# Recurrence blocks opened early, beside products and in a head lane's bank, with attention heads dealt seven and five

## The reference

```python
z = h @ w_in
za, zb, zc = jnp.split(z, [3 * A_WIDTH, 3 * A_WIDTH + 2 * B_WIDTH], axis=-1)
oa = dilated_attention(q, k, v, rel_bias_table)      # 12 heads of 64
ob = spatial_gating(zb, norm_gain, w_s, b_s)         # gelu, layernorm, a 128x128 product per group
oc = rwkv7_time_mix(zc, ...)                         # 12 heads of 64, two to a block of 128 channels: 6 blocks
return jnp.concatenate([rmsnorm(oa), rmsnorm(ob), oc], axis=-1) @ w_out
```

```python
zc = zc + (prev - zc) * mu                           # shift by one token
w_log = -softplus(-(w0 + tanh(w_lo) @ w_up)) - 0.5
decay = exp(-exp(w_log))
a = sigmoid(a0 + a_lo @ a_up)
kk = normalize(k * k_k);  k = k * (1.0 + (a - 1.0) * k_a)
state = state * w_t + sa * (kk_t * a_t) + v_t * k_t;  y_t = state @ r_t
y = layernorm per head(y) * ln_gain + ln_bias + sum(r * k * r_k) * v
return y * g
```

## Time and profile before

| what | us |
|---|---|
| median of three runs | 2358.93 |
| the profiled execution's own time | 2356.4 |
| its span (first to last instruction) | 2354.7 |
| TensorE busy | 2267.6 |
| last stages of products, ST_VB on | 218.75 to 338.24 |
| mixer, first opening | 338.24 to 365.72 |
| mixer, levels to output, blocks 0 to 2 | 365.72 to 452.46 |
| mixer, second opening | 452.46 to 474.48 |
| mixer, levels to output, blocks 3 to 5 | 474.48 to 557.58 |
| last finishes and splits, to the first product of ST_OUT | 557.58 to 565.19 |

### The profile page before, as it was taken

The page is one execution under the profiler, slowest core; times in us unless marked ns, Lnnn a source line. Parts: engine busy times, 40 slices in busy tenths (PEclk is TensorE's granted clock), DMA queues, the critical chain, the costliest instruction groups (busy, mean ns, idle before and its releaser), DMA issues.

```text
span 2354.7 us, 31774 instructions
## 1 busy us (share of the span) xinstructions
PE 2267.6 (96%) x13038; PEld 1971.1 (84%) x13038; DVE 1359.6 (58%) x1694; ACT 1066.1 (45%) x1375; POOL 58.2 (2%) x66
## 2 busy tenths in 40 slices
PE   8999989899989999999999999999998999999998
PEld 7888978788877888888888888888986889889776
DVE  5444657476566766667676444755445555545554
ACT  4433433323455545454555333545435453544543
POOL 0000020011000000000000000000000000000000
PEclk9999998899999999999999999999999999999999
DMA  7656520013634555555565555554550556445243
GB/s 276 198 173 217 185 89 1 1 32 115 220 114 144 191 183 193 182 194 181 194 199 196 193 189 191 191 191 128 186 179 19 179 179 221 161 149 169 68 128 140
DMA packets 235977, 373.07 MB, mean 158 GB/s; under 512 B 8359, under 2 KB 108244, under 8 KB 235092
## 3 DMA queue, kind: packets, MB, share of 16 engines
q1 hardware_dynamic: 229740, 362.89, 46.9%
q10 hardware_dynamic: 6120, 8.50, 1.0%
HBM read 369.25 MB, written 2.12 MB: 158 GB/s over the span
## 4 chain that ended last, share of the span: by engine, by line
PE 65%; issue 5%; DVE 4%; ACT 2%; POOL 0%; DVEq 0%; POOLq 0%; ACTq 0%
PE PS L466 16%; PE PS L425 12%; PE PS L427 12%; PE PS L426 12%; PE PS L469 8%; DVE w_lo L343 1%; PE PS L1960 1%; ACT w_hi L338 1%; PE PS L2050 1%; PE PS L2034 1%; PE PS L1944 1%; PE PS L905 1%; DVE small L1998 0%; PE PS L2725 0%; ACT spare L1972 0%
## 5 line engine op out<-in xcount | busy, mean ns | idle before, releaser
L343 DVE TENSOR_TENSOR w_lo<-raw,w_hi 128x2048 fp32r<-128x2048 f32 (+2 forms) x340 | 766.4, 2254 | 760.5 <-ACT w_hi L338 760.3
L338 ACT ACTIVATE w_hi<-raw 128x2048 fp32r<-128x2048 f32 (+2 forms) x340 | 641.2, 1886 | 850.9 <-PE PS L427 491.3
L466 PE MATMUL PS<-h_both,w_hi 128*128 128x512 f32 x1968 | 536.5, 394 | 2.9 <-DVE h_both L922 1.8
L425 PE MATMUL PS<-w_hi,h_both 128*128 128x512 f32 (+2 forms) x1344 | 514.8, 383 | 11.3 <-DVE h_both L922 4.6
L426 PE MATMUL PS<-w_lo,h_both 128*128 128x512 f32 (+2 forms) x1344 | 507.2, 377 | 0.0
L427 PE MATMUL PS<-w_hi,h_both 128*128 128x512 f32 (+2 forms) x1088 | 408.0, 375 | 0.0
L466 PEld LDWEIGHTS PS<-h_both,w_hi 128*128 128x128 f32 x1968 | 336.5, 188 | 47.4 <-DVE h_both L922 2.8
L469 PEld LDWEIGHTS PS<-h_both,w_lo 128*128 128x128 f32 x1968 | 301.2, 188 | 42.9
L469 PE MATMUL PS<-h_both,w_lo 128*128 128x256 f32 x1968 | 313.1, 281 | 0.0
L425 PEld LDWEIGHTS PS<-w_hi,h_both 128*128 128x128 f32 x1344 | 254.0, 189 | 59.1 <-DVE h_both L922 5.1
L426 PEld LDWEIGHTS PS<-w_lo,h_both 128*128 128x128 f32 x1344 | 254.2, 189 | 45.5
(11 more groups left out here) (523 smaller groups left out, 2045.0 us busy)
## 6 DMA issues: line engine op xcount, KB each, us to landing
raw<-in_w_in SPq DMA_DIRECT2D x132, 1024.0 KB, 5.1
raw<-in_ffn_w_up SPq DMA_DIRECT2D x176, 512.0 KB, 4.3
raw<-in_w_out SPq DMA_DIRECT2D x48, 1024.0 KB, 5.1
raw<-in_ffn_w_down SPq DMA_DIRECT2D x44, 1024.0 KB, 5.0
raw<-in_mem_wkv SPq DMA_DIRECT2D x8, 1024.0 KB, 11.7
raw<-in_mem_wq SPq DMA_DIRECT2D x4, 1024.0 KB, 5.5
raw<-in_mem_wo SPq DMA_DIRECT2D x4, 1024.0 KB, 7.4
raw<-in_w_in SPq DMA_DIRECT2D x4, 768.0 KB, 4.5
```

What stands on the lines that cost most here:

```text
L338: act.activation(w_hi[:, slot % 2, :st.n], raw[:, slot, :st.n], ACT.Copy).then_inc(hi_made, 1)
L343: dve.tensor_tensor(w_lo[:, slot % 2, :st.n], raw[:, slot, :st.n], w_hi[:, slot % 2, :st.n].bitcast(F32), ALU.subtract).then_inc(lo_made, 1)
L425: pe.matmul(ps, l_hi, r_hi, start=start, stop=False, skip_group_check=skip)
L466: pe.matmul(sums, wh[:, k, cs], h_both[:, :, kk, :], start=kk == 0, stop=False, skip_group_check=True)
```

## The change

The opening of a block becomes a job of its own (`open_tensor`, `open_scalar`, `open_vector`, kept in `rk_opens`), and a recurrence block has 19 rounds.

- Openings of blocks 0, 1, 2 are woven in beside products, starting two rounds apart (`EARLY`), in PSUM banks 6, 7 and 5. For this `prepare_*` begins with ST_VB and makes a whole shift per round in another order (`SHIFTS`), the spatial gating starts four rounds after it, and parts of the low-rank weights are loaded early by four more transfers on ScalarE's queue. Evacuations of ST_QK and ST_V0 wait for openings whose scratch room they overwrite (`qk_scalar` and its like).
- Openings of blocks 3, 4, 5 are the first three jobs of head lane 1, six rounds each, in that lane's bank 3: rounds 0 to 17 of the mixer.
- Heads are dealt 0 to 6 to lane 0 and 7 to 11 to lane 1. Lane 0 then has finishes 0 and 2 (rounds 35 to 42), lane 1 has head 11 in rounds 38 to 42, `a_norm` in 43 and finish 1 in 44 to 47. The recurrence lanes have 38 rounds, 0 to 37. The pauses and the early putting aside of four heads are gone.
- Masks are loaded during the last product stage to other places, and GpSimd zeroes the recurrence's matrices and writes their diagonals after one of the last two units.

```diff
+def rounds(n):
+    for _ in range(n):
+        yield
+def after(n, part):
+    yield from rounds(n)
+    yield from part
+def spaced(part, pauses):
+    for n in pauses:
+        yield from rounds(n)
+        next(part, None)
+        yield
...
-        SHIFTS = (18, 15, 12, 0, 3, 6, 9)
+        SHIFTS = (6, 12, 15, 18, 9, 0, 3)
+        V_BANK = 4
...
-        MASKS, PAIR = 6144, 7426
-        GUP, YT, LE = 4096, 6144, (5632, 7680)
-        LNG, LNB = 0, C_W
+        MASKS, PAIR = 5632, 5632
+        GUP, YT, LE = 4096, 6144, ((sp_, 6144), (rw, 7680))
+        LNG, LNB = 4608, 21248
...
+            o = Steps(open_chain if inside else lane["chain"], **OPEN)
...
+            o.room = early_rooms[b] if o.first else dict(kk=lane["kk"], a=lane["a"], L=lane["L"], E=lane["E"],
+                                                         u0=late_u[b - 3][:, 0, :], u1=late_u[b - 3][:, 1, :])
+            o.bank = (6, 7, 5)[b] if o.first else OPEN_BANK
...
+        def qk_scalar(act, q):
+            if q.c == 2:
+                act.wait_ge(rk_opens[0].dve, rk_opens[0]["al"])
+            qk_to_scalar(act, q)
...
+        EARLY = (0, 2, 4)
+
+        def opened(part, e, pauses):
+            return together(*[after(n, spaced(part(e, rk_opens[b]), pauses)) for b, n in enumerate(EARLY)])
+
+        def opened_tensor(pe):
+            return opened(open_tensor, pe, (1, 2, 2, 1))
...
         def recur_tensor(pe, j):
...
-            pe.matmul(PS[:, A, 0:S], raw_flat[0:HD, LORA + j.b * P:LORA + (j.b + 1) * P], zc[0:HD, 18, :], start=True,
-                      stop=True).then_inc(j.pe, 1)
...
-            pe.wait_ge(j.dve, j["al"])
+            pe.wait_ge(j.o.dve, j.o["al"])
...
-        HEADS_FIRST, TO_FIRST, TO_SECOND, HEAD_ROUNDS = 8, 3, 5, 5
-        LANE_JOBS = [[Pause(TO_FIRST)] + side_jobs[0:HEADS_FIRST:2] + [Pause(TO_SECOND)] + side_jobs[HEADS_FIRST::2]
-                     + [finishes[0], finishes[2]],
-                     [Pause(TO_FIRST)] + side_jobs[1:HEADS_FIRST:2] + [Pause(TO_SECOND)] + side_jobs[HEADS_FIRST + 1::2]
-                     + [a_norm, finishes[1]]]
-        PUT_FIRST = (0, 1, HEADS_FIRST, HEADS_FIRST + 1)
+        LANE_JOBS = [side_jobs[:HEADS_FIRST] + [finishes[0], finishes[2]],
+                     [rk_opens[b] for b in range(3, CB)] + side_jobs[HEADS_FIRST:] + [a_norm, finishes[1]]]
...
+        def later_tensor(pe, j):
+            yield from spaced(open_tensor(pe, j), (0, 0, 1, 0))
+            yield
...
-            for st in (ST_C, ST_CE, ST_VB):
+            for st in (ST_C, ST_CE):
                 run(products_tensor(pe, st))
-            fill = prepare_tensor(pe)
-            weave(products_tensor(pe, ST_B1), fill)
-            fill = together(fill, gating_tensor(pe))
-            weave(products_tensor(pe, ST_QK), fill)
-            weave(products_tensor(pe, ST_V0), fill)
+            fill = together(prepare_tensor(pe), after(4, gating_tensor(pe)), after(4, opened_tensor(pe)))
+            for st in (ST_VB, ST_B1, ST_QK, ST_V0):
+                weave(products_tensor(pe, st), fill)
             run(fill)
             mixer(pe, recur_tensor, side_tensor)
...
+            act.dma_start(z_v[0:HD, 0, 0:3 * P], I["rwkv_w_up"][0][:, 0:3 * P]).then_inc(lora_early, 16)
+            act.dma_start(z_v[HD:P, 0, 0:3 * P], I["rwkv_a_up"][0][:, 0:3 * P]).then_inc(lora_early, 16)
...
+            for n, (lane, zero) in enumerate(zip(rk_lanes, zeros)):
+                pool.wait_ge(unit_used, ST_V0.U1 - (2 if n == 0 else 1))
+                pool.memset(lane["mats"], 0.0).then_inc(zero.pool, 1)
...
-            sp.wait_ge(unit_used, ST_V0.U1)
-            sp.dma_start(sp_(MASKS, 8 * P), I["masks"][:, 0:8 * P]).then_inc(masks_in, 16)
+            sp.wait_ge(sgu.dve, sgu["nsq1"])
+            sp.dma_start(ar(MASKS, 8 * P), I["masks"][:, 0:8 * P]).then_inc(masks_in, 16)
+            sp.wait_ge(lo_made, ST_V0.U1 - 1)
```

More of the change, by code:

```diff
@@ L1057, in prepare_scalar @@
         def prepare_scalar(act):
[L1058 to L1061, removed]
+            yield from rounds(4)
+            act.wait_ge(prep.dve, prep["m3"])
             act.activation(zc[0:HD, 18, :], zc[0:HD, 18, :], ACT.Tanh).then_inc(prep.act, 1)
@@ L1163, in gating_vector @@
             st = sgu_stats
-            for n in range(2):
-                yield
-                yield
-            yield
+            yield from rounds(6)
             for t_ in range(TB):
@@ L1266, in hybrid_two_blocks @@
         rk_jobs = {}
+        open_chain = Chain(new, "rk_open")
+        OPEN_BANK = 3
+        OPEN = dict(pe="low lora nsum nbc bonus0 bonus", act="sig_e sig_a sq nb end f0 f1 g0 g1 h0 h1 hh", pool="npow",
+                    dve="l0 l1 kk ka kmod nmax kkn ru akk plus minus end0 end1 bon be kE rg al")
+        late_u = (sp_(7168, 2, S), sp_(7680, 2, S), sp_(2816, 2, S))
+        rk_opens = {}
         for b in range(CB):
@@ new lines, in opened_scalar, with opened_vector, recur_tensor @@
+        def opened_scalar(act):
+            return opened(open_scalar, act, (3, 0, 2, 2, 0))
+        def opened_vector(dve):
+            return opened(open_vector, dve, (3, 0, 1, 2, 2))
+        def recur_tensor(pe, j):
+            lane, A, B, r, k, bs = block_views(j)
+            mats, X, XT, U, bt = (lane[n] for n in ("mats", "X", "XT", "U", "bt"))
+            R, SA, S1, a, kk = lane["R"], lane["SA"], lane["S1"], j.o.room["a"], j.o.room["kk"]
+            zero = zeros[rk_lanes.index(lane)]
+            psA = PS[:, A, :].rearrange("p (i t) -> p i t", i=4)
+            psB = PS[:, B, :].rearrange("p (i t) -> p i t", i=4)
+            if j.first:
+                pe.wait_ge(act_evac, ST_V0.G1)
+                pe.wait_ge(dve_evac, ST_V0.G1)
+                pe.wait_ge(sgu.act, sgu["nsq"])
+                pe.wait_ge(sgu.dve, sgu["x1"])
+                for b in range(3):
+                    pe.wait_ge(rk_opens[b].dve, rk_opens[b]["bon"])
+            else:
+                pe.wait_ge(j.dve, j.dve0)
+                pe.wait_ge(j.act, j.act0)
+            pe.wait_ge(j.o.dve, j.o["al"])
@@ L1547, in recur_vector, with norm_gpsimd @@
             yield
+        def norm_gpsimd(pool, j):
+            pool.wait_ge(j.dve, j["nmax"])
+            power_minus_half(pool, j.norm, 2 * TB).then_inc(j.pool, 1)
         def recur_gpsimd(pool, j):
-            lane = j.lane
-            yield
-            yield
-            pool.wait_ge(j.dve, j["nmax"])
-            power_minus_half(pool, lane["norm"], 2 * TB).then_inc(j.pool, 1)
-            yield
-            for _ in range(6):
-                yield
-            for l in range(1, 7):
-                yield
-                yield
-            for _ in range(4):
-                yield
+            yield from rounds(22)
         def by_head(ap):
@@ L1756, in dilated_vector @@
             yield
[L1757 to L1758 removed]
+            put_aside(dve, j)
         def put_aside(dve, j):
@@ L1764, in put_aside @@
             dve.wait_ge(j.dve, j["recip"])
+            if h in (0, HEADS_FIRST):
+                for b in range(3):
+                    dve.wait_ge(rk_opens[b].dve, rk_opens[b]["al"])
             for t_ in range(TB):
@@ L3036, in lanes_made, with mixer @@
                 e.wait_ge(j.dve, j.dve1)
-        def mixer(e, recur, side, first=iter(())):
-            run(together(first, *[one_by_one([recur(e, rk_jobs[b]) for b in (i, i + 3)]) for i in range(3)],
+        def mixer(e, recur, side):
+            run(together(*[one_by_one([recur(e, rk_jobs[b]) for b in (i, i + 3)]) for i in range(3)],
                          *[one_by_one([side(e, j) for j in jobs]) for jobs in LANE_JOBS]))
```

488 lines of the change are left out of this document (268 added, 220 removed).

## The result

The changed kernel is slower: median 2370.31 us against 2359.54 (8 runs each, 2364.89 to 2373.38 against 2355.99 to 2361.82), a ratio of 1.0045 with a 95% interval of 1.0034 to 1.0056. The forecast was 2351, with a range from 2336 to 2364.

What follows compares the result with a forecast made beforehand. TensorE, busy 2267.6 of 2354.7 us, and its standstills were taken to bound the kernel. Removed stretches, second-pass savings and added costs summed to −8.1 us: 2348.3, plus 2.5 for the median, rounded to 2351; range 2336 to 2364.

Steps and rivals of the forecast that it cites:

- Beside products: Openings of blocks 0 to 2 woven in beside products: +9 us, with ends +4 and +16.
- The pairs at once: First pass's pairs follow the last product after some 0.9 us of latency, which takes away 26.6 us.
- The tail: Between last recurrence output and first product of ST_OUT: 27.5 us instead of 7.61, +20.9 with the lower clock.
- Its small term: First product of ST_OUT: TensorE leaves the tail at the lower clock, about 1 us more than today.
- The passes: Last product to last output: opening stretches −26.6 and −22.0, heads +4.8 and +4.85, openings +5.4, stalls +8, second-pass savings.
- three spots: Stalls inside the levels: norm sum in round 1, 2 us; round of `al`, 1.7; round starting the state, 4.2.
- What the second pass gains: Second pass: −3.6 us waits, −1.6 and −1.7 slow matmuls, −1.8 finish gates, −3.8 head work moved to the tail.
- What the openings cost inside the levels: Openings of blocks 3 to 5 among the recurrence levels: +8 us of stalls, between 0 and 22.
- the stalls inside the levels are large: Rival: opening steps wait on TensorE's in-order list round after round; from 16 us of stalls, likely 2364; chance 0.15.
- my sign of being wrong: Wrong if stalls in the first 18 rounds sum to over 16 us, or the tail is under 20.
- The argument against it: Between an opening's steps lies a round of over 3 us, about the longest waits of today's openings, 3.85 and 2.96.

## Why the prediction was wrong

*Beside products: the sum right (+9.3, forecast +9) by luck, the parts wrong.* I had 5.4 us of TensorE, 2 of self-waits and broken runs, and 1.5 of a wait at the gelu. There was no such wait. The openings' matmuls took about 7.6 us by their starts, self-waits in it; the rest are transposes (0.7 us more than before) and broken runs of products (0.6). The low-rank pair is what I took too small, as these rows beside products show:

```profile
234.57 0.70 PE L1346 MATMUL PS<-arena 64*128 64x256 f32 x2
235.33 0.70 PE L1348 MATMUL PS<-arena 64*128 64x256 f32 x2
```

In the kernel before, L1315 took 0.45 us with L1317 started 0 to 0.04 us after it, about 0.5 for a block. Now both write one bank, the second waits for the first, and they take 0.70 each, 1.46 for a block from 234.57 on. `nsum`, `nbc` and the bonus, for which I had 0.4, 0.5 and 0.4, took 0.37, 0.42 and 0.36. The table loads cost 1.28 us each: the one at 436.42 ends at 437.70, and the next instruction starts at 437.71, as in the earlier trace rows. The Trainium skill ("ScalarE: Activation LUTs", What ACT_TABLE_LOAD costs) has 2.66 us with the drain; the trace disagrees here too, and it decides.

*The pairs at once: right.* 0.83 us after the last product, forecast 0.9.

*The tail: right.* 28.05 us, forecast 27.5. Its steps came at 9.7 (head 11 put aside), 13.0 (norm), 19.5 (finish 1) and 28.05; I had 10.1, 13.6, 18.8 and 27.5. Its small term, 1 us because TensorE comes out of the tail at the lower clock, was wrong: the first product of ST_OUT takes 0.50 us where it took 0.73, at a granted clock of 1.00 over the next 10 us for 0.83 before. That gains nothing either: 23.16 us after that product's start both kernels have issued 103 matmuls, and the changed one has waited for 1.1 us.

*The passes: wrong, and this is the error.* From the last product to the last output I forecast 219.3 − 38.0 = 181.3 us; it was 200.5. Of these 19.2 us, the windows put 6.9 on idle time and 12.3 on busy time.
- Idle. The three spots that I named were right in place and nearly in sum: 3.91 for 2, 2.33 for 1.7, 3.48 for 4.2, together 9.7 for 8. (At the last of them 2.08 us stand even without an opening in the lanes, with the exponentials of two heads.) I left out smaller ones (0.95, 0.48, 0.77) and the new wait in the second pass, 3.08 us, in which head scores stand behind the masked copies. The step that failed here is "What the second pass gains": I let 3.6 us of waits go and looked for none in their place. The second pass stands still for 6.35 us where it did for 6.5.
- Busy, the larger part. The step that failed is "What the openings cost inside the levels": its +8 priced the waits as idle time alone, with nothing for slow matmuls behind them, and I let 1.6 and 1.7 us of slow matmuls go besides. The granted clock was 0.94 and 0.96 instead of 0.99 and 0.97. Read as a share at half clock, that is 20.3 us of the passes instead of 6.7, which makes up to 6.8 us more busy time where I had 3.3 less: up to 10.1 of the 12.3 (the clocks are read to two places, so this is an estimate). The rest, 2.2, is about what three low-rank pairs at 1.4 us instead of 0.5 add, 2.7, less the little that the other matmuls of an opening took less.

The rival "the stalls inside the levels are large", to which I gave 0.15, had the mechanism, but not the price. It was to decide from 16 us of stalls, and my sign of being wrong was over 16 in the first 18 rounds. The new waits of those rounds sum to 11.9 us, and to 15.5 with those of the second pass. What carried the time past 2364 was the slow clock, up to 7 us on top, which neither the rival nor the forecast had. The argument against it, that a whole round lies between two steps of an opening, failed at the first opening. A round measured on TensorE is no measure for VectorE and ScalarE, which had 3.9 us of masked copies and a head's softmax in that round. The experiments show it: with one more round for the norm sum of block 3 alone, and the others a round later, −9 us, of which 5.6 are that lead.

What the experiments say of the parts: openings beside products gain 6.7 us alone. Openings in the head lane with enough lead, and with the side jobs dealt as in the change, give that gain back (2361.35): against the early openings alone the second opening's 23.5 us are gone, but the second pass is 11.6 us longer with the displaced heads, and the tail 21.3. With the tail shortened the whole is some 9 us lower (ratio 0.9970 for 1.0008).

## What to carry to other kernels

When a step moves from a stretch of its own in among lanes that run in lockstep, count its lead on the engines that make its operand, with everything in their lists, not in rounds of the engine that waits; one round too few cost 5.6 us here. Price a wait of 2 us or more on TensorE with slow matmuls behind it, as a likely cost and not a certain one. And add up the rounds of side jobs before moving more into a side lane: what doesn't fit under the main lanes comes back as a serial tail, and what stands there last should be what the next product needs.

## What the runs showed of the hardware

Low-rank products over 64 rows each, on different halves of the partitions and into different banks, start together and take about 0.5 us for a block; the same into one bank, the second waiting for the first, take 1.46. Whether the bank or only the wait makes this was not tried.

TensorE ran at its lower clock level after waits of 2.33, 3.08, 3.48 and 3.91 us in the changed kernel, after 2.49 us in the kernel before, and after 3.45 us with all openings a round later. It stayed at the upper level after 2.23 us with the norm sum one round later and after 1.79 us with all openings a round later. Short waits close together can do the same (four of 0.37 to 0.77 us ahead of 430.55). What decides between these cases was not tried.
